# A hybrid S5, short-convolution and mixture-of-experts model: the lag blocks of the scan's matrix in four 32-partition strips of one bank, and modulation sums and constants moved to other stages

## The reference, cut to what matters

```python
mod = cond @ ada_w[i] + ada_b[i]              # cond = silu(c), one row
sh1, sc1, g1, sh2, sc2, g2 = jnp.split(mod, 6, axis=-1)
hn = modulate(rmsnorm(x, norm1_g[i]), sh1, sc1)
# s5_mixer: u = hn @ w_in, 64 groups of 16 channels, 64 complex states each
#   h[t] = a * h[t-1] + B u[t];  y[t] = Re(C h[t]) + d * u[t]
#   y = gelu(y); val, gate = split(y @ w_glu); out = val * sigmoid(gate)
x = x + (1 + g1) * out
hn = modulate(rmsnorm(x, norm2_g[i]), sh2, sc2)
x = x + (1 + g2) * hier_moe(hn, ...)
```

## Time and profile before

| | before |
|---|---|
| device time, median of 3 runs (range) | 7016.55 us (7015.04 to 7017.35) |
| the profiled execution's own time | 7015.28 us |
| its span | 7013.7 us |
| PE, PEld busy | 91%, 75% |
| DVE, ACT, POOL busy | 47%, 29%, 21% |
| mean granted TensorE clock | 0.956 |
| moved by DMA | 1073 MB, 153 GB/s over the span |

### The profile page before, as it was taken

One profiled execution on the slowest core, in us unless ns is written; L12 is line 12 of the kernel. 1 busy time (PEld: TensorE's weight loads), 2 busy tenths in 40 slices (PEclk: granted clock), 3 DMA queues, 4 the chain that ended last, 5 costly groups with the idle time before them and its releaser, 6 DMA issues. The chain is left out here.

```text
span 7013.7 us, 90561 instructions
## 1 busy us (share of the span) xinstructions
PE 6407.3 (91%) x30729; PEld 5236.7 (75%) x30730; DVE 3326.9 (47%) x4885; ACT 2051.1 (29%) x3301; POOL 1448.3 (21%) x1250
## 2 busy tenths in 40 slices
PE   6997888799996999999997999998998699999994
PEld 1876667588884788888886888886776588888883
DVE  4445666343336555555643422222545654466554
ACT  1112443222221343343433500000111243344434
POOL 0001222488002232222321000000000322232222
PEclk8998999899998999999998999999998899999997
DMA  6221111444222676676754544433334365677766
GB/s 205 66 87 46 48 50 48 158 142 144 85 84 79 199 223 178 186 215 200 225 157 149 194 178 166 148 135 137 133 131 141 117 189 167 191 217 237 222 200 244
DMA packets 528270, 1073.08 MB, mean 153 GB/s; under 512 B 59550, under 2 KB 137374, under 8 KB 527146
## 3 DMA queue, kind: packets, MB, share of 16 engines
q1 hardware_dynamic: 425364, 805.88, 33.6%
q0 software_dynamic: 69888, 249.12, 14.1%
q10 hardware_dynamic: 32920, 16.80, 0.8%
HBM read 816.33 MB, written 255.38 MB: 153 GB/s over the span
## 5 line engine op out<-in xcount | busy, mean ns | idle before, releaser
L127 PE MATMUL conv_p<-conv_x_lo,conv_w_hi 128*128 128x512 f32 x1536 | 601.1, 391 | 0.0
L128 PE MATMUL conv_p<-conv_x_hi,conv_w_lo 128*128 128x512 f32 x1536 | 598.5, 390 | 0.0
L129 PE MATMUL conv_p<-conv_x_hi,conv_w_hi 128*128 128x512 f32 x1536 | 598.3, 390 | 0.0
L1758 DVE SCALAR_TENSOR_TENSOR m_o<-m_pO,m_weight_of,m_gate 128x512 f32<-128x512 f32 x320 | 237.0, 746 | 726.6 <-POOLq L1398 376.6
L1725 DVE TENSOR_TENSOR m_w_lo<-m_w_raw,m_w_hi 128x1024 fp32r<-128x1024 f32 x496 | 577.6, 1214 | 0.0
L1533 ACT ACTIVATE m_xT_hi<-m_pX 128x512 fp32r<-128x512 f32 x320 | 191.6, 599 | 1151.9 <-PE m_pB L129 994.2
L127 PE MATMUL m_pA<-m_w_lo,m_xT_hi 128*128 128x512 f32 x1280 | 517.0, 404 | 5.7 <-DVE m_xT_lo L1736 5.7
L1474 PE MATMUL m_pO<-m_w_lo,m_hT_hi 128*128 128x512 f32 x1280 | 512.8, 401 | 0.5 <-ACT m_hT_hi L1538 0.5
L1521 ACT ACTIVATE m_w_hi<-m_w_raw 128x1024 fp32r<-128x1024 f32 x512 | 505.3, 1053 | 0.0
L129 PE MATMUL m_pA<-m_w_hi,m_xT_hi 128*128 128x512 f32 x1280 | 503.0, 393 | 0.0
L128 PE MATMUL m_pA<-m_w_hi,m_xT_lo 128*128 128x512 f32 x1280 | 499.9, 391 | 0.0
(11 more groups left out here) (354 smaller groups left out, 12702.6 us busy)
## 6 DMA issues: line engine op xcount, KB each, us to landing
m_w_raw<-in_moe_w_dram SPq DMA_DIRECT2D x384, 1024.0 KB, 7.3
conv_x_hi<-hT_hi SPq DMA_DIRECT2D x24, 2048.0 KB, 9.3
conv_x_lo<-hT_lo SPq DMA_DIRECT2D x24, 2048.0 KB, 13.9
mod_w<-in_ada_w_dram SPq DMA_DIRECT2D x12, 2048.0 KB, 7.8
glu_ada<-in_ada_w_dram POOLq DMA_DIRECT2D x96, 256.0 KB, 3.1
a_x<-in_x_dram SPq DMA_DIRECT2D x32, 512.0 KB, 3.5
u<-a_stage POOLq DMA_DIRECT2D x4, 4096.0 KB, 19.2
s_u<-u SPq DMA_DIRECT2D x64, 256.0 KB, 2.6
```

What stands on the lines that cost most here:

```text
L127: pe.matmul(out, lh, rl, start=start, stop=False)
L128: pe.matmul(out, ll, rh, start=False, stop=False)
L129: return pe.matmul(out, lh, rh, start=False, stop=stop)
L1758: dve.scalar_tensor_tensor(out=ob[:, n, :], in0=pO[:, n, :], scalar=wslot[:, bass.ds(tile_, 1)], in1=gate2[:, n, :], op0=ALU.mult, op1=ALU ...
```

## The change

The code before and after differ in all four phases. (1) `ssm_tables` computes only the first 2048 values of the modulation (shift and scale of the first norm), in four chunks with a buffer each, behind the parameter loads; `cond` and the bias are loaded from ACT's queue, the skip vector by POOL in four small DMAs in another layout, and POOL adds the bias and stores. (2) `ssm_input` computes the other 4096 values with the same kind of partial sums on POOL, as eight chunks of eight steps, two chunks ahead of each store of the stage; at the end SP loads the eight partial sums (2 MB) over the weights, PE adds over the partitions with a column of ones (8 products), ACT copies and stores. Its three constants go through POOL's queue, and `w_in` is loaded and split in eight pieces of 2 x 128 rows by 512 columns. The stage is written in reversed time order inside a block of eight, and the scan's tables `back_r` and `back_i` are turned accordingly. (3) `ssm_scan` computes only the first 16 rows of R (the lag blocks) for each group: one product of 512 columns with a table z that is zero except for 16 of 32 columns, whose result fills 32 partitions of a bank pK; the four groups' products stand together in `inner` of the last group. DVE takes the bank once for a batch (`out_k`, behind the last matrices), SP stores it (256 KB) behind 112 zero columns, waits, and loads each R with a shifted access pattern (4 x 256 KB). (4) `project` issues its constants from POOL, after the sixth weight piece has landed, loads the weights in pieces of one product bank (`glu`: 4 x 128 rows by 512 columns, `cout`: 2 x 128 rows by 512), and DVE waits for the constants behind the splits. The sums on POOL use three buffers, not four.

`Modulation` and the new `PartialSums`:

```diff
-    ROUNDS = MOD // HALF // 2
+    CHUNKS = 2 * D // HALF
...
     def loads(self, sp):
+        for q in range(self.CHUNKS):
+            sp.dma_start(self.w[q][:], self.w_view[:, :, bass.ts(q, HALF)]).then_inc(self.w_ld[q], 16)
...
+    def biases(self, pool):
...
+class PartialSums:
...
+    def run(self, pool, first, end):
+        for n in range(first * KD, end * KD):
+            q, k, s = n // KD, n % KD, n % self.SLOTS
+            pool.wait_ge(self.ld[s], 16 * (n // self.SLOTS) + 16)
+            if k == 0:
+                pool.wait_ge(self.bias, 16 * q + 16)
+                if q >= 1:
+                    pool.wait_ge(self.st, 16 * q)
+            pool.tensor_scalar(self.buf[s][:], self.buf[s][:], self.cond[:, 1, k:k + 1], None, ALU.mult).then_inc(self.step, 1)
+            pool.wait_ge(self.step, 2 * n + 2)
+            pool.tensor_tensor(self.acc[:], self.buf[s][:], self.zero[:] if k == 0 else self.acc[:], ALU.add) \
+                .then_inc(self.step, 1)
...
+            if n + self.SLOTS < self.chunks * KD:
+                self.load(pool, n + self.SLOTS)
+            if k == KD - 1:
+                pool.dma_start(self.out[q], self.acc[:]).then_inc(self.st, 16)
```

`ssm_input`:

```diff
-def ssm_input(core, ident, x, norm_g, w_in, mod_dram, u_dram):
+def ssm_input(core, ident, x, norm_g, w_in, mod_dram, u_dram, cond, ada_w, ada_b, partial):
...
+            n, k = q // 4, 2 * (q % 4)
+            return w[:, k:k + 2, n * HALF:(n + 1) * HALF]
...
+            sp.wait_ge(part_ready, 1)
+            for s in range(2):
+                sp.wait_ge(mm[s], 2 + NT)
+            sp.dma_start(part.rearrange("p (q n) -> p q n", n=HALF), partial[0:PARTS].rearrange("q p n -> p q n")).then_inc(p_ld, 16)
...
+            pool.dma_start(gain[:], row(norm_g[0:1, :], 0, D)).then_inc(const_ld, 16)
+            load_mod(pool, mod_dram, 0, SC1, scale[:], const_ld)
+            load_mod(pool, mod_dram, 0, SH1, shift[:], const_ld)
+            pool.memset(ones[:], 1.0).then_inc(ones_set, 1)
+            later.clear(pool)
+            later.start(pool)
             pool.sem_inc(stage_free, 1)
-            with pool.Fori(0, NT // BLK) as n:
+            for n in range(NT // BLK):
+                later.run(pool, PARTS * n // (NT // BLK), PARTS * (n + 1) // (NT // BLK))
                 pool.wait_ge(blk_ready, BLK * n + BLK)
-                pool.dma_start(u_view[bass.ds(n, 1)].squeeze(0), stage[:]).then_inc(blk_stored, 16)
-                pool.wait_ge(blk_stored, 16 * n + 16)
-                pool.sem_inc(stage_free, 1)
+                pool.dma_start(u_view[n], stage[:]).then_inc(blk_stored, 16)
+                if n + 1 < NT // BLK:
+                    pool.wait_ge(blk_stored, 16 * n + 16)
+                    pool.sem_inc(stage_free, 1)
+            later.finish(pool)
+            pool.sem_inc(part_ready, 1)
...
+            pe.wait_ge(ones_set, 1)
+            pe.wait_ge(p_ld, 16)
+            for q in range(PARTS):
+                if q >= 4:
+                    pe.wait_ge(p_out, q - 3)
+                pe.matmul(sum_of(q), ones[:], part[:, q * HALF:(q + 1) * HALF], start=True, stop=True).then_inc(p_mm, 1)
...
+            for q in range(PARTS):
+                act.wait_ge(p_mm, q + 1)
+                act.activation(part_out[:, q * HALF:(q + 1) * HALF], sum_of(q), ACT.Copy).then_inc(p_out, 1)
+            act.wait_ge(p_out, PARTS)
+            act.dma_start(mod_dram[0:1, FIRST:], part_out).then_inc(p_st, 16)
+            act.wait_ge(p_st, 16)
```

`ssm_tables`:

```diff
-            mod.first_loads(sp)
...
-            for i in range(SB):
-                get(tab.skip[i * CH:(i + 1) * CH, :], d_skip[0].rearrange("(g c) -> c g", c=CH), True)
...
+            for i in range(4):
+                pool.dma_start(tab.skip[32 * i:32 * i + CH, :], d_skip[0].rearrange("(b i c) -> i c b", i=4, c=CH)[i],
+                               allow_slow_non_contiguous=True).then_inc(skip_ld, 16)
...
+            mod.biases(pool)
...
-            mod.products(pe, 0, 1)
...
+            mod.products(pe)
```

`ssm_scan`:

```diff
+            def toeplitz(i, s):
+
+                b = 2 * i + s
+                sp.wait_ge(k_out, b + 1)
+                sp.dma_start(k_dram[s][:, PAD:], ks[s][:]).then_inc(k_st[s], 16)
+                sp.wait_ge(k_st[s], 16 * i + 16)
+                for g in range(BG):
+                    moved = bass.AP(tensor=k_dram.tensor, offset=(s * P + g * LANES) * (PAD + L * CH),
+                                    ap=[[CH, SB], [PAD + L * CH, CH], [1, L * CH]])
+                    sp.dma_start(flat(R[s][g][:]), moved).then_inc(r_ld[s], 16)
+
+            sp.wait_ge(zeroed, BG + 2)
+            for s in range(2):
+                sp.dma_start(k_dram[s][:, 0:PAD], pad[:]).then_inc(pad_st[s], 16)
+            load(0, 0, (0, 1))
+            def body(i, first, last):
+                for s in range(2):
+                    load(i, s, (2, 3))
+                    if not (last and s == 1):
+                        load(*at(i, s, 1), (0, 1))
+                    toeplitz(i, s)
+            pairs(sp, NB // 2, body)
 
...
-            def out_r(i, s, g):
-                n = number(i, s, g)
-                dve.wait_ge(r_psum, n + 1)
-                r = flat(R[s][g][:])
-                dve.scalar_tensor_tensor(out=r[:, 0:P], in0=ident[:], scalar=tab.skip[:, bass.ds(n, 1)],
-                                         in1=flat(pR[:])[:, 0:P], op0=ALU.mult, op1=ALU.add)
-                dve.tensor_copy(r[:, P:], flat(pR[:])[:, P:]).then_inc(r_out, 1)
+            def out_k(i, s):
+                b = 2 * i + s
+                dve.wait_ge(k_psum, b + 1)
+                dve.wait_ge(k_st[s], 16 * i)
+                dve.scalar_tensor_tensor(out=ks[s][:, 0:CH], in0=diag[:], scalar=tab.skip[:, bass.ds(b, 1)],
+                                         in1=pK[:, 0:CH], op0=ALU.mult, op1=ALU.add)
+                dve.tensor_copy(ks[s][:, CH:], pK[:, CH:]).then_inc(k_out, 1)
...
                     if g + 1 < BG:
                         table_o(i, s, g + 1)
                         out_p(i, s, g + 1)
-                    out_r(i, s, g)
                     if g + 2 < BG:
                         table_p(i, s, g + 2)
                     matrices(i, s, g)
+                out_k(i, s)
...
-                pe.wait_ge(r_out, n + 1)
+                if g < BG - 1:
+                    return
+                pe.wait_ge(b_ready, n + 1)
                 pe.wait_ge(tab_o, n + 1)
-                o, r = flat(O[s][g][:]), flat(pR[:])
-                for j in range(SB):
-                    pe.matmul(r[:, j * CH:P], flat(z[q][:])[:, (SB - 1 - j) * CH:(SB - 1 - j) * CH + P],
-                              o[:, 0:(SB - j) * CH], start=j == 0, stop=False, skip_group_check=True)
-                pe.matmul(r[:, P:], flat(pt[q][:])[:, (KB - 1) * P:], o[:, CH:CH + (KB - 1) * P],
-                          start=False, stop=True, skip_group_check=True).then_inc(r_psum, 1)
+                pe.wait_ge(k_out, 2 * i + s)
+                for g_ in range(BG):
+                    lanes = slice(g_ * LANES, (g_ + 1) * LANES)
+                    last = pe.matmul(pK[lanes, :], z[g_][:, lanes], flat(O[s][g_][:])[:, 0:L * CH], start=True, stop=True)
+                last.then_inc(k_psum, 1)
...
             def inside(i, s, g):
...
-                pe.wait_ge(r_out, n + 2)
+                if g == 0:
+                    pe.wait_ge(r_ld[s], 16 * BG * (i + 1))
```

`project`:

```diff
+        KQ = NB_
+
+        def piece(w, q):
+
+            b, k = order[q * KQ // KD], q * KQ % KD
+            return w[:, k:k + KQ, b * HALF:(b + 1) * HALF]
...
-            sp.dma_start(gate1[:], row(mod_dram[layer:layer + 1, :], G1 * D, D)).then_inc(const_ld, 16)
...
             load_src(0, 0)
             load_src(0, 1)
-            for k in range(KD):
-                sp.dma_start(w_raw[:, k, :], w.rearrange("(k p) n -> k p n", p=P)[k]).then_inc(w_ld[k], 16)
-            load_x(0, 0)
+            for q in range(KD):
+                sp.dma_start(piece(w_raw, q), piece(w.rearrange("(k p) n -> p k n", p=P), q)).then_inc(w_ld[q], 16)
+                if q == 1:
+                    load_x(0, 0)
...
+        @block.gpsimd
+        def _(pool):
+            pool.wait_ge(w_ld[KD - 3], 16)
+            constants_of(pool)
...
-            dve.wait_ge(const_ld, 8 * 16)
...
             low(0, 0)
-            for k in range(KD):
-                dve.wait_ge(w_hi_ready, k + 1)
-                dve.tensor_tensor(w_lo[:, k, :], w_raw[:, k, :], w_hi[:, k, :].bitcast(F32), ALU.subtract) \
+            for q in range(KD):
+                dve.wait_ge(w_hi_ready, q + 1)
+                dve.tensor_tensor(piece(w_lo, q), piece(w_raw, q), piece(w_hi, q).bitcast(F32), ALU.subtract) \
                    .then_inc(w_split, 1)
+            dve.wait_ge(const_ld, 8 * 16)
+            c = Chain(dve, step)
+            fold_scale(dve, c, gain[:], hn[0][:])
+            c(dve.tensor_scalar(gate1[:], gate1[:], 1.0, None, ALU.add))
...
```

(52 more changed lines are left out.)

246 lines of the change are left out of this document (119 added, 127 removed).

## The result

| | before | after |
|---|---|---|
| device time, median (range) | 7015.8 us (7014.7 to 7017.4, 4 runs) | 6900.7 us (6898.1 to 6903.0, 4 runs) |
| ratio, with its 95% interval | | 0.9836 (0.9821 to 0.9852) |
| the profiled execution's own time, its span | 7015.28, 7013.7 us | 6898.08, 6896.5 us |
| tables, to the first load of input | 134.2 us | 84.5 us (-49.7; forecast -56) |
| input, to the first memset of the scan | 447.4 us | 465.8 us (+18.4; forecast +12) |

The change saves 115 us, where 93 were forecast. The time lies in the range, outside the likeliest case's own (6905 to 6945) and inside that of the rival *strips side by side* (6884 to 6902). First the windows of the three phases after, to be held against the earlier trace rows; the columns are the same.

What follows compares the result with a forecast made beforehand. No engine filled every phase: tables had no full engine, PE limited input, and scan alternated between DVE's chain and PE. Terms -56 + 12 - 16 - 27 - 6 = -93 took 7015.3 to 6922 us, range 6880 to 6958.

Steps and rivals of the forecast that it cites:

- likeliest case: Whole kernel: the five priced places sum to -93 us, giving 6922, own range 6905 to 6945; chance 0.57.
- strips side by side: Rival, scan: PE's lag blocks take 2.2 or 0.9 us, not 3.6; 20 to 38 us less, 6884 to 6902; chance 0.25.
- late POOL: Rival, input, glu, cout: POOL slowed by sharing with DVE, PE stalls at three blocks, constants late; 6974; chance 0.13.
- the tables are not shortened: Rival, tables: parameter loads held by the queue itself, chain starts as late as before; 6932 to 6940; no separate chance.
- 3.6 because the nearest row, L885, has the same columns and type: Scan: four lag products priced as 8 instructions one after another, 0.45 us each, 3.6 us a batch.
- none of them, -2 a batch, -28: Scan, a bound: if no batch has a fall of the clock, 2 us a batch less, -28 us.
- clock, slower: Rival, scan: PE idles early, clock at 1.2 GHz for later work; 20 us a batch more, 7200; chance 0.03.
- The wait for R: Scan: DVE's wait for R, 0.71 us, counted within 2.2 us a batch that DVE's chain saves.
- net of -0.7 a batch: Scan: 2.2 us saved on DVE's chain, 1.9 shared-port gain, +1.2 for PE's lag blocks; -10 over 14 batches.
- 54 us: Tables: chain's length from landing of the parameters; starting at 22.5 it ends at 76.5, next phase at 78, -56 us.
- 0 together: Input's start: constants through POOL's queue 1 to 3 us longer, first tile gains about 2; between -2 and +3.
- The tail: Input's end: partial sums' loading (15 to 20 us), 8 products, last copy and store; +12 us, between +5 and +20.

Runs made afterwards that it cites:

- full-width run: The kernel after, each lag product using the whole 128-column table z and accumulating over all 128 partitions, not a 32-partition strip each: 6936.8 us, ratio 0.9889.
- filled kernel before: The kernel before with unused 512-column products in PE's waits for the P table, one for group 2 and two for group 3: 6994.0 us, ratio 0.9971.
- run with early constants: The kernel after, but in glu and cout POOL issues the constants when the second weight piece has landed, not the sixth: 6900.1 us, ratio 0.9839.

## Why the prediction was right, and where it was not

**Right.** Direction, range, and four of the five places where the time would change (cout changed by nothing). Of the five terms two lie outside their own bounds, the tables (-50, from -51 to -61) and the scan (-62, from -60 to +30). The tables end on the chain and not on the modulation; the next phase begins 1.1 us behind it (forecast 1.5). POOL keeps up in input, so *late POOL* did not happen, and the chain's start did move, so neither did *the tables are not shortened*. glu's start was within a microsecond (39.9 against 39). In cout the moved constants are the last wait, as said.

**Scan, -62 for -16.** This step failed, and its largest term is the rival *strips side by side*: the choice of "3.6 because the nearest row, L885, has the same columns and type". It came as the rival's lower end, 1.00 us a batch and not 3.6 (0.9 was the bound). The full-width run puts 31.5 us of the distances and 5.8 of the first batch on it, 37 of the 46 that are missing. The Trainium skill's "Part 3: Packing small matmuls" in "TensorE: Matmul & The Clock Gate" says that products in different 32-partition strips run at once; this trace agrees (1.00 us for four strips). What "TensorEngine Tiling (Array Packing)", "Key Properties", says of a drain at a change of mode has at most a small price here. Behind the strips it is 1.00 less two rounds of 0.43, 0.14 us; ahead of them the lag products start 1.06 us behind the eight products before them (802.65, 803.71) and 0.96 in the full-width run (773.66, 774.62), 0.10 more. That both are the drain is not shown.

The other 9 us are the balance of larger terms. Two I took from the cheap form of a batch:
- *The clock.* I had "none of them, -2 a batch, -28" only as an edge of the range. The falls didn't go, they became more (7 us or more at half clock in ten of the 14 distances, where eight had 3.4 or 6.8 and six none), but they moved into the stretch where DVE sets the pace. By the filled kernel before, the falls had cost (42.92 - 41.67) x 14 = 17.5 us; the kernel after pays little of it. The rival *clock, slower* had seen rightly that PE would idle more, and had put the fall in the wrong half of the batch.
- *The wait for R.* I priced it at 0.71 from the earlier trace rows; every second batch it was 1.83, behind the store of y. With R gone this lateness is covered too: 1.2 x 7 = 8 us.

Two go the other way. The net of -0.7 a batch was too good: with full-width products the cheap distance is 41.05 against 41.13, so 0.1 less and 9 us worse than forecast. And the first batch gave 7.4 us as a whole (forecast 6), but 5.8 of them by the strips, so its own part is 4 us short. Then falls that last up to the lag products still cost some 3 us (distances of 38.9 to 39.8 in place of 38.8): 17.5 + 8 - 9 - 3 - 4 = 9.5, for the 9 that were missing.

**Tables, -50 for -56.** The term "54 us" for the chain was right for the old chain. I priced the 4 additions on POOL at nothing, though I took a loss from POOL and DVE working together in the scan: 3.7 us, shown by taking them away. The parameters came at 25.9, not 22.5, inside the bounds of 18 and 27; in the other traces of this phase they came between 23.0 and 26.3, and why is open.

**Input, +18 for +12.** "0 together" at the start was the error. The two halves are measured: 3.7 us for the constants through POOL's queue and 7.1 for POOL's sums beside DVE's first tiles. Together this start is outside its bounds of -2 to +3. I had looked at whether DVE slows POOL, not at whether POOL slows DVE where DVE leads. The tail was 6.4 us, less than the 12: its 8.6 us for the sums and 2.8 for the seam are close to the forecast, but their transfer took 12.3 us beside the store, not 15 to 20.

**cout, 0 for -6.** The second tile's products came 30.0 us behind the first load and not 27: 3.6 us earlier than in the kernel before (33.6). Of these 3.0 went at once. The sum had no term for the clock behind PE's wait for the constants, and the tile took 17.9 us from its start to the next where the kernel before has 14.8 at the full clock:

```profile
4909.06:4923.90 14.84, 13.73 (x74) 11.56 (x72) 11.06 (x12) 2.27 (x4) 0.00 (x0) 1.00 0.43 144
```

The run with early constants shows the same tile without that wait, at 14.9. In glu the second tile's products begin 26.3 us earlier than before (41.5 for 67.8 us behind the first load), and 24.6 of them are left at the first load of the expert phase. The 0.8 us that are then lost up to cout's first load stand in phases that the change doesn't touch; why is open.

Had the strips not run side by side, the same kernel would have taken 6937 us: the forecast of 6922 would then have been 15 too low. The misses have both signs, and that the total is 21 off says little about its terms.

## What to carry to other kernels

Float32 products with at most 32 output rows are worth bringing together: four, each into its own 32-partition strip, took 1.00 us where the same four over all partitions took 3.44. Ask of an idle stretch not whether the clock will fall behind it but which engine leads while it is down: a fall in a stretch that another engine led was free here, and filling the waits pushed the fall to where it cost. Where PE itself leads behind the wait, as in cout's second tile, the clock is part of the wait's price. Work given to a free engine can be paid by its neighbour: here POOL's additions and sums cost time where DVE led. Start such work behind that stretch.

## What was not expected of the hardware

- A 1 x 512 addition on POOL (1.25 to 1.69 us) held one DVE operation each: 0.22 became 0.89, 1.23 became 2.17, 0.27 became 1.32, 0.69 became 1.73. That is 3.7 us for four additions on a single partition; it looks as if DVE had waited for the rest of POOL's operation (POOL 46.57 to 48.26, DVE 47.17 to 49.34).
- The eight instructions of four strips all start within 0.5 us of each other and last 0.6 us each; the group takes 1.00 us.
- Behind a wait of PE of 6.3 us in cout the clock was 0.83 over the next tile, which took 17.9 us and not 14.9.
- With 2.7 us of unused work in each of two waits of 3 us, the clock still fell in eight of the 14 distances, only later. What decides the place of the fall is open.
